# Where the page decays of a sample attention are summed, and which engine scales its low output rows

## What is computed

```python
cum_f = jnp.cumsum(logf_all, axis=1)
s = jnp.einsum('bqhd,bkhd->bhqk', qi, k) * scale
s = s + cum_f_query - cum_f_key          # masked where k_pos > q_pos
p = jax.nn.softmax(s, axis=-1)
out = jnp.einsum('bhqk,bkhd->bqhd', p, v)
```

```python
k_past = cache_k[l][page_table].reshape(bs, past_len, A_HEADS, A_HEAD_DIM)
f_past = cache_logf[l][page_table].reshape(bs, past_len, A_HEADS)
```

## Time and profile before

| what | us |
| --- | --- |
| median of 3 runs | 3920.55 (3910.69 to 3921.47) |
| the profiled execution | 3914.49 |
| its span, first to last instruction | 3912.8 |
| TensorE matmuls busy over the span | 3672.9 (94%), 19019 instructions |
| VectorE busy | 1848.9 (47%), 3047 |
| ScalarE busy | 1680.2 (43%), 3409 |
| GpSimd busy | 1078.9 (28%), 764 |
| transfers | 590.75 MB, mean 151 GB/s |

### The profile page before, as it was taken

One profiled execution on the slowest core, in us unless ns is written; L12 is line 12 of the kernel. 1 busy time (PEld: TensorE's weight loads), 2 busy tenths in 40 slices (PEclk: granted clock), 3 DMA queues, 4 the chain that ended last, 5 costly groups with the idle time before them and its releaser, 6 DMA issues. The chain is left out here.

```text
span 3912.8 us, 55757 instructions
## 1 busy us (share of the span) xinstructions
PE 3672.9 (94%) x19019; PEld 2972.9 (76%) x19019; DVE 1848.9 (47%) x3047; ACT 1680.2 (43%) x3409; POOL 1078.9 (28%) x764
## 2 busy tenths in 40 slices
PE   8999999999999999996999996888799999799999
PEld 7788888887788888885877885666577777588887
DVE  3234433223134533323434443877788888644532
ACT  4224434455234424432443442555567676421222
POOL 0011233120011222201000001556577777422200
PEclk9999999999999999997989998989899999899999
DMA  4224333333233343324010003788799999644422
GB/s 158 97 97 131 127 137 130 105 127 121 94 115 127 113 158 131 120 86 117 1 44 12 1 12 126 235 273 270 244 320 330 323 330 324 241 167 159 165 86 84
DMA packets 354281, 590.75 MB, mean 151 GB/s; under 512 B 44029, under 2 KB 90213, under 8 KB 354026
## 3 DMA queue, kind: packets, MB, share of 16 engines
q1 hardware_dynamic: 340722, 576.00, 43.7%
q10 hardware_dynamic: 12736, 9.32, 0.8%
q0 software_dynamic: 576, 2.10, 0.1%
HBM read 475.38 MB, written 111.96 MB: 150 GB/s over the span
## 5 line engine op out<-in xcount | busy, mean ns | idle before, releaser
L853 PE MATMUL prj_z_ps<-prj_w_hi,prj_h_hi 128*128 128x512 f32 x2312 | 924.0, 400 | 2.8 <-DVE prj_w_lo L677 2.8
L855 PE MATMUL prj_z_ps<-prj_w_hi,prj_h_lo 128*128 128x512 f32 x2312 | 902.6, 390 | 0.0
L854 PE MATMUL prj_z_ps<-prj_w_lo,prj_h_hi 128*128 128x512 f32 x2312 | 901.2, 390 | 0.0
L1688 POOL TENSOR_TENSOR sa_v_lo<-sa_v_raw,sa_v_hi 128x1024 fp32r<-128x1024 f32 x256 | 615.9, 2429 | 324.6 <-DVE sa_v_hi L1859 324.6
L855 PEld LDWEIGHTS prj_z_ps<-prj_w_hi,prj_h_lo 128*128 128x128 f32 x2312 | 434.4, 188 | 93.8
L853 PEld LDWEIGHTS prj_z_ps<-prj_w_hi,prj_h_hi 128*128 128x128 f32 x2312 | 435.3, 188 | 89.7 <-DVE prj_w_lo L677 5.5
L854 PEld LDWEIGHTS prj_z_ps<-prj_w_lo,prj_h_hi 128*128 128x128 f32 x2312 | 435.5, 188 | 84.7
L1853 DVE TENSOR_TENSOR sa_kT_lo<-sa_t_ps,sa_kT_hi 128x512 fp32r<-128x512 f32 x512 | 345.1, 685 | 182.2 <-ACT sa_kT_hi L1718 178.0
L2027 PE MATMUL sa_t_ps<-sa_ident,sa_k_raw 128*128 128x128 f32 x2048 | 314.7, 285 | 92.3 <-DVE sa_kT_lo L1853 89.4
L2027 PEld LDWEIGHTS sa_t_ps<-sa_ident,sa_k_raw 128*128 128x128 f32 x2048 | 251.8, 146 | 176.2 <-DVE sa_kT_lo L1853 107.7
L1718 ACT CAST sa_kT_hi<-sa_t_ps 128x512 fp32r<-128x512 f32 x512 | 293.7, 590 | 178.5 <-PE sa_t_ps L2027 167.0
(11 more groups left out here) (310 smaller groups left out, 5872.1 us busy)
## 6 DMA issues: line engine op xcount, KB each, us to landing
sa_k_raw<-in_cache_k_dram SPq DMA_DIRECT2D x512, 256.0 KB, 3.9
sa_v_raw<-in_cache_v_dram SPq DMA_DIRECT2D x512, 256.0 KB, 4.0
prj_w_raw<-in_w_main_dram SPq DMA_DIRECT2D x272, 256.0 KB, 4.0
z_scratch<-prj_z_sb SPq DMA_DIRECT2D x272, 256.0 KB
mo_mg<-z_scratch SPq DMA_DIRECT2D x51, 512.0 KB, 3.8
prj_cu<-extp_scratch SPq DMA_DIRECT2D x48, 256.0 KB
pa_raw<-z_scratch SPq DMA_DIRECT2D x12, 1024.0 KB, 10.7
prj_x_in<-in_x_all_dram SPq DMA_DIRECT2D x17, 512.0 KB, 3.7
```

Of the source, the lines that this page charges most:

```text
L853: pe.matmul(out, h_hi[:, slot_of(t), k], hi, start=(k == 0), stop=False)
L854: pe.matmul(out, h_hi[:, slot_of(t), k], lo, start=False, stop=False)
L855: mm = pe.matmul(out, h_lo[:, slot_of(t), k], hi, start=False, stop=(k == KC - 1))
L1688: pool.tensor_tensor(v_lo[:, w % 2, at], v_raw[:, w % RING, at], v_hi[:, w % 2, at].bitcast(F32), ALU.subtract).then_inc(vlo_ready, 1)
```

## The change

- The decays of the past pages are summed in `attend_prompt`. GpSimd builds `later` there and gathers one group per pair of heads (`gather`); VectorE does the eight scans of a group in steps j = 0 to 7 of query group 1 of the even head, and the page sums, the rest and the three passes in steps j = 0, 4, 5, 7 and 9 of group 2 (`past`); TensorE's matmul with `later` is at j = 2, into `t_ps[:, 1]`, and the last turn of the group waits until it has been read. SP stores the results (`store_past`) and loads the page numbers between the loads of pair 0 and pair 1.
- `attend_sample` has no groups any more. `load_d` for chunks 0 and 1 stands at the very start of ScalarE's list.
- Of the set-up, the mask, the decays of the new keys and `lift_r` move from ahead of step 0 into step 1; `third_pass` waits for `lift_r`.
- `o_low` is scaled by ScalarE (`divide_low`) at the end of c = 5, the combination stays on VectorE and moves from c = 4 to c = 5, and `finish` moves from c = 5 to c = 6.

The diff, cut to its core:

```diff
+def attend_prompt(nc, z, decay_key, y_a, cache_logf, page_table, decay_past):
...
+        page_of = m.sb("page_of", [P, HEADS // 2], I32)
+        lf = m.sb("lf", [P, PAGE * HEADS])
+        cum = m.sb("cum", [P, HEADS, PAGE])
+        whole = m.sb("whole", [P, HEADS])
+        rest = m.sb("rest", [P, HEADS])
+        d_hi = m.sb("d_hi", [P, HEADS, PAGE], F32R)
+        later = m.sb("later", [P, P])
...
                 do.score(h, hh, n)
+                if hh == 0:
+                    do.past(h, g, j)
...
+            past = decay = turn = maximum = negate = score = weigh = lambda self, *where: None
...
+            def store_past(group):
+                pages = slice(group * P, (group + 1) * P)
+                sp.wait_ge(past_step, 3 * group + 3)
+                sp.dma_start(decay_past[pages, 0:HEADS], d_hi[:].bitcast(F32)).then_inc(past_stored, 16)
+                sp.dma_start(decay_past[pages, HEADS:2 * HEADS], cum[:]).then_inc(past_stored, 16)
...
             load(0, 0)
+            with nc.allow_non_contiguous_dma(reason="512 words"):
+                sp.dma_start(page_of[:], page_table.rearrange("(g s) n -> (s n) g", s=IN_GROUP)).then_inc(past_stored, 16)
             load(1, 1)
...
+                store_past(pair)
                 store(pair)
             sp.wait_ge(stored, 16 * (HEADS // 2))
+            sp.wait_ge(past_stored, 16 + 32 * (HEADS // 2))
...
+            def gather(group):
+                pool.wait_ge(past_stored, 16)
+                wait_from(pool, past_step, 3 * group)
+                pool.indirect_dma_start(lf[:], None, cache_logf.rearrange("l n k h -> (l n) (k h)"),
+                                        bass.IndirectOffsetOnAxis(ap=page_of[:, group:group + 1], axis=0)).then_inc(gathered, 16)
+                pool.wait_ge(gathered, 16 * (group + 1))
             for h in range(HEADS):
                 prepare(h, h % 2, h // 2, h // 2 % 2)
+                if h == 1:
+                    pool.memset(later[:], 1.0).then_inc(later_made, 1)
+                    pool.wait_ge(later_made, 1)
+                    pool.affine_select(out=later[:], in_=later[:], compare_op=ALU.is_gt, fill=0.0, base=0,
+                                       pattern=[[-1, P]], channel_multiplier=1).then_inc(later_made, 1)
+                    pool.wait_ge(later_made, 2)
+                    by_seq = later[:].rearrange("p (s n) -> p s n", s=IN_GROUP)
+                    pool.affine_select(out=by_seq, in_=by_seq, compare_op=ALU.is_ge, fill=0.0, base=N_PAGES - 1,
+                                       pattern=[[N_PAGES, IN_GROUP], [0, N_PAGES]], channel_multiplier=-1).then_inc(later_made, 1)
+                    gather(0)
+                elif h >= 2 and h % 2 == 0:
+                    gather(h // 2)
...
+                def past(self, h, g, j):
+                    if g == 1:
+                        if j == 0:
+                            dve.wait_ge(gathered, self.pair * 16 + 16)
+                            dve.wait_ge(past_stored, self.pair * 32 + 16)
+                        by_head = lf[:].rearrange("p (k h) -> p h k", h=HEADS)[:, j]
+                        dve.tensor_tensor_scan(cum[:, j], by_head, by_head, 0.0, ALU.add, ALU.bypass).then_inc(scanned, 1)
+                    if g != 2:
+                        return
+                    log_rest = lf[:].rearrange("p (h k) -> p h k", h=HEADS)
+                    wide = rest[:].unsqueeze(2).broadcast_to([P, HEADS, PAGE])
+                    if j == 0:
+                        dve.wait_ge(scanned, self.pair * HEADS + HEADS)
+                        dve.tensor_copy(whole[:], cum[:, :, PAGE - 1]).then_inc(whole_ready, 1)
+                    if j == 4:
+                        dve.wait_ge(later_summed, self.pair + 1)
+                        dve.tensor_tensor(rest[:], t_ps[:, 1, 0:HEADS], whole[:], ALU.add).then_inc(rest_ready, 1)
+                    if j == 5:
+                        dve.wait_ge(rest_ready, self.pair + 1)
+                        dve.tensor_tensor(log_rest, wide, cum[:], ALU.subtract).then_inc(past_step, 1)
+                    if j == 7:
+                        dve.tensor_tensor(d_hi[:], wide, cum[:], ALU.subtract).then_inc(past_step, 1)
+                    if j == 9:
+                        dve.wait_ge(past_step, self.pair * 3 + 2)
+                        dve.tensor_tensor(cum[:], log_rest, d_hi[:].bitcast(F32), ALU.subtract).then_inc(past_step, 1)
...
+                def past(self, h, g, j):
+                    if g == 2 and j == 2:
+                        pe.wait_ge(later_made, 3)
+                        pe.wait_ge(whole_ready, self.pair + 1)
+                        pe.wait_ge(max_set, h * GROUPS + 2)
+                        pe.matmul(t_ps[:, 1, 0:HEADS], later[:], whole[:], start=True, stop=True).then_inc(later_summed, 1)
                 def turn(self, h, hh, c):
+                    if c == 2 * GROUPS + 3 and hh == 0:
+                        pe.wait_ge(rest_ready, self.pair + 1)
...
-            pool.wait_ge(page_loaded, 16)
-            log_rows = cache_logf.rearrange("l n k h -> (l n) (k h)")
-            for g in range(GROUPS):
-                pool.indirect_dma_start(lf[:, g], None, log_rows,
-                                        bass.IndirectOffsetOnAxis(ap=page_of[:, g:g + 1], axis=0)).then_inc(gathered[g], 16)
-                if g == 0:
-                    then(pool.memset(ident[:], 0.0))
-                    select(ident[:], 1.0, ALU.not_equal, 0, [[-1, P]])
-            then(pool.memset(later[:], 1.0))
-            select(later[:], 0.0, ALU.is_gt, 0, [[-1, P]])
-            select(later[:].rearrange("p (s n) -> p s n", s=IN_GROUP), 0.0, ALU.is_ge, N_PAGES - 1,
-                   [[N_PAGES, IN_GROUP], [0, N_PAGES]], -1)
+            then(pool.memset(ident[:], 0.0))
+            select(ident[:], 1.0, ALU.not_equal, 0, [[-1, P]])
             then(pool.memset(lift[:], 0.0))
...
-            for g in range(GROUPS):
-                pool.wait_ge(gathered[g], 16)
...
-            def store_d(group):
-                pages = slice(group * P, (group + 1) * P)
-                act.wait_ge(past_step, 3 * group + 3)
-                act.dma_start(decay_past[pages, 0:HEADS], d_hi[:].bitcast(F32)).then_inc(d_stored, 16)
...
+            def divide_low(n):
+                act.wait_ge(sum_step, 6 * n + 6)
+                act.wait_ge(kept, (n + 1) * PER)
+                wait_from(act, o_ready, n)
+                act.mul(o_low[:], o_acc[R:P], recip[R:P, 0:1]).then_inc(low_ready, 1)
...
+            load_d(0)
+            load_d(1)
             act.wait_ge(pre_turned, 1)
             act.mul(qT[:], heads_of(t_ps[:, 0])[:, :, 0:SAMPLE], HEAD_DIM ** -0.5).then_inc(pre_scalar, 1)
             act.wait_ge(pre_turned, 2)
             act.copy(kn_hi[:], heads_of(t_ps[:, 1])[:, :, 0:SAMPLE]).then_inc(pre_scalar, 1)
-            act.wait_ge(mask_done, 1)
-            act.copy(mask[:].rearrange("p n t -> p (n t)"), x_ps[0:R]).then_inc(mask_ready, 1)
...
-                if g == 1:
-                    store_d(0)
-                    act.wait_ge(new_step, 3)
-                    act.dma_start(dn_raw[0:HEADS], new_hi[:].bitcast(F32)).then_inc(dn_loaded, 16)
-                    act.dma_start(dn_raw[HEADS:2 * HEADS], new_neg[:]).then_inc(dn_loaded, 16)
-                    act.wait_ge(d_stored, 32)
-                    load_d(0)
-                    load_d(1)
...
+                if g == 1:
+                    act.wait_ge(mask_done, 1)
+                    act.copy(mask[:].rearrange("p n t -> p (n t)"), x_ps[0:R]).then_inc(mask_ready, 1)
+                    act.wait_ge(new_step, 3)
+                    act.dma_start(dn_raw[0:HEADS], new_hi[:].bitcast(F32)).then_inc(dn_loaded, 16)
+                    act.dma_start(dn_raw[HEADS:2 * HEADS], new_neg[:]).then_inc(dn_loaded, 16)
...
-                group, at = group_of(g)
-                if at == 8:
-                    store_d(group)
-                    act.wait_ge(d_stored, 32 * (group + 1))
                 if c == 5 and 1 <= n <= DEC_BATCH:
+                    divide_low(n - 1)
+                if c == 6 and 1 <= n <= DEC_BATCH:
                     finish(n - 1)
...
             def divide(n):
                 dve.wait_ge(sum_step, 6 * n + 6)
                 dve.wait_ge(kept, (n + 1) * PER)
-                wait_from(dve, o_ready, n)
-                dve.tensor_scalar(o_low[:], o_acc[R:P], recip[R:P, 0:1], None, ALU.mult).then_inc(low_ready, 1)
                 dve.wait_ge(low_ready, n + 1)
...
-            dve.wait_ge(gathered[0], 16)
-            for h in range(HEADS):
-                scan(0, h)
-            whole_of(0)
...
-            rest_of(0, p_ps[:, 0:HEADS])
-            for i in range(3):
-                past(0, i)
-            dve.wait_ge(new_summed, 1)
-            dve.tensor_scalar(new_neg[:], p_ps[0:HEADS, P:P + SAMPLE], -1.0, None, ALU.mult).then_inc(new_step, 1)
-            dve.wait_ge(new_step, 1)
```

(46 more changed lines are left out.)

68 lines of the change are left out of this document (12 added, 56 removed).

## The result

The changed kernel takes 3806.7 us (median of 4 runs, 3806.07 to 3810.66) against 3915.6 for the kernel before beside it (4 runs): ratio 0.9727, 95% interval 0.9701 to 0.9753. The forecast was 3810 us, with a range of 3788 to 3843. The profiled span went from 3912.8 to 3804.3 us.

What follows compares the result with a forecast made beforehand. TensorE paced the prompt attention; in the sample attention VectorE's queue held up TensorE early, TensorE and transfers shared the bound late. -91.4 - 18.2 + 3.5 - 9 + 5 = -110.1 us, from 3920.55 to 3810 us, range 3788 to 3843.

Steps and rivals of the forecast that it cites:

- Groups, -91.4: Sample attention: taking the decay groups out of three early samples' steps saves 91.4 us, bounds 80 and 97.
- Division, -18.2: Sample steps: o_low on ScalarE and division one step later save 2.6 us, seven times, 18.2 us; between 3 and 21.
- +3.5 for the sends: A sample's eight output sends, one step later on ScalarE, cost 0.5 us more for each of seven; bounds -7 and +8.
- a hit: o_sb runs at the border between GpSimd's two v_lo halves; forecast to ask 0.3 us before it and take near 0.74.
- a miss: o_sb misses the border and waits for GpSimd's second v_lo half; forecast bound 2.6 + 0.3 us for one division.
- The second rival: o_sb inherits the lock wait, border missed each time: 2.2 us more, seven times, 3825 us; chance 0.22.
- Set-up, -9: Sample stage set-up: work removed ahead of the first keys and work moved into step 1 save 9 us, between 3 and 14.
- 8 + 6.6 + 2 and the wait of -4: Set-up terms: first key turn 8 us earlier, store wait of 6.57 gone, step 0 2 shorter, new wait about 3 to 4.
- the -3.6: Set-up term: mask and new sums now on the path in step 1 cost 3.6 us.
- Prompt, +5: Prompt attention: added scans, passes and matmul cost 1.3 us per pair, times 4, +5 us; bounds 3 and 28.
- The clock rival: Prompt stage: TensorE loses its clock in even heads, up to 74 us more each, 4101 us; chance 0.03.
- Transfers hold the pace: Late samples: the ring can't give 334 GB/s, period stays at 104.1, 15 us less gain, 3825 us; chance 0.08.

Runs made afterwards that it cites:

- the repeat: The changed kernel run once more, unaltered, beside the kernel before; ratio 0.9730.
- the PSUM run: Against the changed kernel: o_low written to free columns of the x_ps bank, o_sb in two instructions with one operand from PSUM; ratio 0.970.
- a set-up put back: Against the changed kernel: mask, new tokens' decays and cast of the lift matrix ahead of the first keys again; ratio 0.9718, set-up 33.9 us for 37.2.
- the work twice: Against the changed kernel: each prompt scan and two of three whole-tile passes run a second time on VectorE; prompt stage 613.5 us against 603.5 to 607.8.
- the sum behind the cast: Against the changed kernel: o_sb issued in step 6 directly behind the cast v_hi, not at the end of step 5; steps 4 to 9 10 to 14 us less.
- the last experiment: Against the changed kernel with half of GpSimd's low-value subtraction: TensorE's product cut to the same half; a sample 99.9 to 96.4 us, time another 28 us less.
- the two other kernels without the change: The kernel before with ScalarE's store wait four steps later, or with group scans and passes directly behind the cast; 0.7 and 0.5% under the kernel before.

## Why the prediction was right, and where only its sum was

*Groups, -91.4: right.* 91.05 measured by itself, with a spread of some 4. The argument by ticks (the late samples are the same code without the groups) held; the split that I left open is 18 wait, 24 place, 49 not separated.

*Division, -18.2 with +3.5 for the sends: mis-sized.* Per sample steps 4 to 9 went from 34.7 in an undisturbed sample to 32.2 in a hit (2.5 less; 2.1 forecast) and 34.1 in a miss (0.6). In sum 9 to 13 us, nearer 9. The step that failed is the margin of 0.3 us from the earlier trace rows, on which the 0.7 us for one division rested. In sample 3 o_low took 0.72 us, not 0.6, the hand-over to VectorE 0.20 (2764.44 to 2764.64), not 0.1, and GpSimd's second half began 2.34 us behind the first, not 2.38; with the rest of a few hundredths this used up the 0.3, and o_sb came 0.01 late. The second rival, o_sb inheriting the wait, to which I gave 0.22, is what five of seven samples did (six in the repeat). It cost about 9 us, not 15, since a miss still replaces two waits by one. The rule of the Trainium skill behind that rival (SBUF — State Buffer, "SBUF: two separate sides") is borne out by the PSUM run: with one operand of two out of SBUF there was no wait inside the pair.

*Set-up, -9: right in size and nearly so in its parts.* 10 to 11.5 us measured. Its rows have to be counted from the stage's first instruction, which comes at 2408.34 before and at 2410.25 after. So counted, I put the first key turn at 10.0 us, and it came at 10.6 for 18.2 before: 7.6 us less for my 8. What ended its wait was the landing of its keys (2.10 us), a bound that I had not looked at. Without the reorder the group's removal was worth 14 (48.6 to 33.9 and 34.9), where my terms 8 + 6.6 + 2 and the wait of -4 make 12.6. The reorder costs 3 to 4 us, as the -3.6 said. So what the prediction missed here is no term but the question behind it: the same work ahead of the keys would have cost nothing. The expectation that a set-up put back would be longer came from a wrong reading of that sum, which gave the 6.6 and the 2 to the reorder; they belong to the group.

*Prompt, +5: too much.* 1.3 us per even head were forecast, and the last even head, where it can be seen, shows 0.3. The stage as a whole came out at about -2, with a spread of 4 between executions, because with the change one even head is often short. The second and third even heads took 77.2 to 79.8 us or 74.2 to 74.7. The short form came in none of the three profiles with the stage as before and in seven of the ten with the change, in one head each. With the work twice it did not come either; against the two kernels with the change and no short head at all (607.8 and 605.9 us) the second portion costs 6 to 8 us. In the changed kernel that head (from 2125.62 on) has a granted clock of 0.95; the same head in the repeat, 78.8 us long, has 0.89. Why it comes is open. The clock rival was forecast as a loss; if anything it is a small gain.

*Transfers hold the pace: wrong.* A sample of 16 steps came down to 102.9 us in the changed kernel and to 100.8 with the sum behind the cast, where this rival held it at 104.1, and the last experiment has the transfers at 359 GB/s. *Early steps slow for another reason: wrong*, by the ticks.

*Not forecast:* the two stretches of code that is the same in both kernels came out 10 us longer together. Ahead of the prompt stage it is 4.1, where the profiles of the two other kernels without the change are as long as those with it (1801.6 to 1806.9 us without, 1804.5 to 1809.3 with). Behind the last tick of values it is 5.7: 544.4, 544.4 and 547.0 us in the three profiles without the change, 544.4 to 550.3 in the eleven with it. Most of this is spread between executions; a small share of the change in it is not ruled out. Also, the forecast started from a median of 3920.55, and the kernel before measured 3915.6 beside the changed one. The miss in division, the surplus in the set-up and the prompt, and this spread cancelled: 3807 for 3810 is closer than the terms were, and that is luck.

## What to carry to other kernels

An operation moved to another engine does not take the lock away from its consumer: look at what the consumer reads, and put it where the other engine is known to be idle (directly behind the instruction that this engine waits for), or put one operand in PSUM. A place that fits by 0.3 us on paper doesn't fit. Work in the shadow of a transfer that everybody waits for was free here, and moving it behind the transfer cost 3 to 4 us. Where the same code runs once with and once without the work in question, the difference of the two tells its price better than the sum of its instructions.

## What the runs showed that I had not expected

- Two operands in SBUF or one decides between 2.8 and 0.96 us (0.61 + 0.35) for the same sum at the same moment of GpSimd's pair.
- At the border of two queued GpSimd instructions VectorE got in between when it started 0.06 us or more before the second (2563.22), five times of five, and not when it started from 0.01 us before it to 0.24 after, 23 times of 23.
- A DMA share of 1.00 at 343 GB/s was no limit: the same transfers ran at 359 with a shorter step, at a share of 1.03.
- A matmul into 64x256 took 281 ns where one into 64x512 took 396 (as the profile models them).
- 6.5 us of added VectorE work cost a head of 69 us 0.3 us; another 5.8 cost it 1.6.
